# Depthwise convolution of 31 taps as banded block matmuls over four token phases, in a decoder step on eight cores

## The reference

```python
h = rms_norm(x, g_mix)
z = h @ w_in                                   # 2048 -> 10752 columns
glu = z[..., :2048] + b_glu
u = glu[..., :1024] * sigmoid(glu[..., 1024:])
# conv branch: 31 taps back in time, one filter for each of 1024 channels
uc = concatenate([u_past, u], axis=1)
y = depthwise_conv(uc, w_dw) + b_dw            # y[t, c] = sum_j uc[t + j, c] * w_dw[j, c]
y = silu(layer_norm(y, ln_g, ln_b))            # over the 1024 channels
conv_out = y @ w_pw + b_pw
# and q, k, v with rotary positions, three dilated attentions, their mix o_att
x = x + (sigmoid(z_gc) * conv_out + sigmoid(z_ga) * (o_att @ w_o_att)) @ w_out
x = x + (silu(hf @ w_gate) * (hf @ w_up)) @ w_down      # hf = rms_norm(x)
```

## Time and profile before

| | |
|---|---|
| median of three runs | 2172.33 us |
| the profiled execution | 2170.49 us |
| span of its slowest core (core 1), first to last instruction | 2168.6 us |
| spans of the eight cores | 2164.3 to 2168.6 us |
| granted TensorE clock, share of full, each core | 0.989 to 0.990 |
| TensorE matmul busy | 2060.5 us, 95% |
| VectorE / ScalarE busy | 706.2 us, 33% / 432.2 us, 20% |

### The profile page before, as it was taken

The page is one execution under the profiler, slowest core; times in us unless marked ns, Lnnn a source line. Parts: engine busy times, 40 slices in busy tenths (PEclk is TensorE's granted clock), DMA queues, the critical chain, the costliest instruction groups (busy, mean ns, idle before and its releaser), DMA issues.

```text
span 2168.6 us, 34938 instructions; the slowest of 8 cores (2164.3 to 2168.6 us)
## 1 busy us (share of the span) xinstructions
PE 2060.5 (95%) x13809; PEld 1277.3 (59%) x13809; DVE 706.2 (33%) x1105; ACT 432.2 (20%) x783; POOL 68.5 (3%) x122
## 2 busy tenths in 40 slices
PE   1599998999999999999999999999999999999997
PEld 0455554665554566666688756565565565665653
DVE  2344334322222332222224332413414314224125
ACT  2533323332222421111103200000010000000013
POOL 0000000000000000000000000000000000000000
PEclk9799999999999999999999999999999999999999
DMA  9144223427849776894382647585495564553423
GB/s 241 64 103 99 55 50 78 101 60 137 144 90 161 126 145 146 126 202 86 59 199 49 120 76 118 84 141 100 83 155 89 92 101 75 88 83 58 80 47 150
DMA packets 43947, 230.91 MB, mean 106 GB/s; under 512 B 5163, under 2 KB 17563, under 8 KB 28403
## 3 DMA queue, kind: packets, MB, share of 16 engines
q0 software_dynamic: 27552, 137.37, 39.9%
q1 hardware_dynamic: 16235, 91.31, 16.4%
HBM read 350.31 MB, written 59.99 MB: 189 GB/s over the span
## 4 chain that ended last, share of the span: by engine, by line
PE 93%; DMA 2%; ACT 2%; DVE 2%; issue 1%; SPq 0%; DVEq 0%; ACTq 0%
PE ps L125 93%; DVE arena L125 2%; ACT arena L125 2%; DMA arena<-xext 1%; DMA arena<-state 1%; ACT L125 0%; SPq L142 0%; DMA y<-arena 0%; DVEq L85 0%; ACTq L85 0%; SPq L85 0%
## 5 line engine op out<-in xcount | busy, mean ns | idle before, releaser
L125 PE MATMUL ps<-arena 128*128 128x512 bf16 (+8 forms) x13809 | 2060.5, 316 | 94.2 <-DVE arena L125 72.1
L125 PEld LDWEIGHTS ps<-arena 128*128 128x128 bf16 (+2 forms) x13809 | 1277.3, 101 | 876.9 <-issue 116.4
L125 DVE TENSOR_TENSOR arena<-ps,arena 128x512 f32<-128x512 f32 (+5 forms) x729 | 413.6, 570 | 912.5 <-PE ps L125 718.2
L125 ACT ACTIVATE arena<-ps 128x347 f32<-128x347 f32 (+2 forms) x285 | 133.6, 478 | 1074.2 <-PE ps L125 1072.7
L125 ACT ACTIVATE arena<-arena 128x2048 bf16<-128x2048 f32 (+6 forms) x140 | 111.8, 804 | 161.5 <-DVE arena L125 137.3
L125 DVE TENSOR_TENSOR arena<-arena 128x1040 f32<-128x1040 f32 (+7 forms) x167 | 122.8, 742 | 35.7 <-ACT arena L125 22.0
L125 DVE SCALAR_TENSOR_TENSOR arena<-ps,arena 128x347 f32<-128x347 f32 (+3 forms) x75 | 43.4, 579 | 275.3 <-PE ps L125 263.0
L125 ACT COPY arena<-ps 128x512 bf16<-128x512 bf16 (+7 forms) x154 | 93.1, 620 | 126.2 <-PE ps L125 124.6
L125 DVE SCALAR_TENSOR_TENSOR arena<-arena 128x2048 bf16<-128x2048 f32 (+5 forms) x36 | 79.2, 2201 | 50.5 <-ACT arena L125 47.6
L125 ACT CAST arena<-ps 128x384 bf16<-128x384 f32 x72 | 37.0, 514 | 178.2 <-PE ps L125 176.6
L125 ACT ACTIVATE arena<-ps,arena 128x357 f32<-128x357 f32 (+4 forms) x42 | 21.6, 515 | 141.1 <-PE ps L125 139.9
(11 more groups left out here) (14 smaller groups left out, 24.3 us busy)
## 6 DMA issues: line engine op xcount, KB each, us to landing
arena<-wgu POOLq DMA_DIRECT2D x44, 1024.0 KB, 10.6
arena<-wgate POOLq DMA_DIRECT2D x16, 1408.0 KB, 17.8
arena<-w_down POOLq DMA_DIRECT2D x11, 2048.0 KB, 25.7
arena<-xext SPq DMA_DIRECT2D x19, 1024.0 KB
arena<-wqkv POOLq DMA_DIRECT2D x9, 2048.0 KB, 22.5
kso<-ck SPq DMA_DIRECT2D x16, 1022.0 KB
vso<-cv SPq DMA_DIRECT2D x16, 1022.0 KB
arena<-wglu POOLq DMA_DIRECT2D x8, 1024.0 KB, 10.4
```

The source lines that it names most:

```text
L125: self.q[eng].append(lambda e, meth=meth, a=a, kw=kw, s=s: getattr(e, meth)(*a, **kw).then_inc(s, 1))
```

## The change

- The convolution. Each 128-channel block is cut into four groups `q` of 32 channels. `glu` writes `u` split in four phases (token mod 4, `uph`), and 16 small DMAs in `glu_end` bring it to a layout in which the partitions are 4 phases x 32 channels (`uP`). Then a 128x128 matrix holds, for a shift of `s` groups of four tokens, the taps between every input and output phase (a block Toeplitz matrix, diagonal in the channels). `conv(n)` becomes 4 groups x 9 shifts = 36 matmuls of 256 columns. The matrices are made on DVE: four multiplies of 128x1152 per block, from `w4` and a mask.
- The sample tokens are convolved on DVE: a multiply, a reduction and a bias of 496 or 16 elements per block.
- The layer norm works in that order (sums with a block matrix `bones`), and 16 DMAs per block bring its output back to `cT`, which now holds the phases one after the other: 256 prompt and 4 sample tokens for each. `gate_mm` part 2 therefore reads `cT` with a step of 260 elements between neighbouring columns.
- The start: identity and gain row are loaded ahead of the first tile, the gain row is spread over the partitions by four matmuls instead of a DMA, each GLU weight load on POOL waits for a tile to have landed, the tables come in final layout (no transposes in `consts`), and two GLU blocks (n = 0 and 1) run inside the tile phase, after tiles 2, 5 and 9.
- The loop goes over n = 2 to 7 with seven halo tiles (two in n = 6); the last convolution moves behind the first q projection of group 2.

The core of the diff:

```diff
@@ glu_end
-            S.op('dve', lambda e: e.tensor_tensor(out=dgv[ui][:, :, :], in0=mkap(identb, [[0, 31], [1, 128]]),
-                                                  in1=mkap(vecT[:, R_WDW + n:R_WDW + n + 1], [[8, 31], [0, 128]]), op=ALU.mult),
-                 ['identb', 'vecT'], ['dg%d' % ui])
+            S.op('act', lambda e: e.copy(out=phases(uph[ui], 186, 78), in_=tok4(u_[:, 0:312])), [uk], [pk])
+            S.op('dve', lambda e: e.tensor_scalar(out=phases(uph[ui], 0, 8), in0=tok4(u_[:, 328:360]), scalar1=hv, scalar2=None, op0=ALU.mult), [uk, 'hv'], [pk])
+            for q in range(4):
+                for f in range(4):
+                    S.dma('sp', uP[ui][32 * f:32 * f + 32, q, :], uph[ui][32 * q:32 * q + 32, f, :], reads=[pk], writes=[Pk])
+            S.op('act', lambda e: e.copy(out=ucb[ui][:, :, 30:34], in_=u_[:, 312:328].rearrange("p (s j) -> p s j", j=4)), [uk], [uc])
+            prod = mkap(sqt[:, 0:1], [[124, 4], [31, 4], [1, 31]])
+            S.op('dve', lambda e: e.tensor_tensor(out=prod, in0=mkap(ucb[ui][:, 0, 0:1], [[34, 4], [1, 4], [1, 31]]), in1=mkap(vecT[:, R_WDW + n:R_WDW + n + 1], [[0, 4], [0, 4], [8, 31]]), op=ALU.mult),
+                 [uc, 'vecT'], ['sqt'])
...
+            for q in range(4):
+                S.op('dve', lambda e: e.tensor_tensor(out=v3(tpw[ui][q], 36), in0=mkap(dmask[:, 0:1], [[0, 36], [1, 32]]), in1=mkap(w4n[:, 36 * q:36 * q + 1], [[1, 36], [0, 32]]), op=ALU.mult),
+                     ['dmask', 'w4'], ['tp%d' % ui])
@@ conv
-            for j in range(31):
-                S.op('pe', lambda e: e.matmul(PS[3][:, :], lhsT=dgv[ui][:, j, :], rhs=ubb[ui][:, j:j + 512], start=(j == 0), stop=(j == 30)),
-                     [dkey_, ukey], [PSK[3]])
...
+            for hf in range(2):
+                bk = 3 + hf
+                for q2 in range(2):
+                    q = 2 * hf + q2
+                    for s in range(9):
+                        S.op('pe', lambda e: e.matmul(PS[bk][:, 256 * q2:256 * q2 + 256], lhsT=tpw[ui][q][:, 128 * s:128 * s + 128], rhs=uP[ui][:, q, s:s + 256], start=(s == 0), stop=(s == 8)),
+                             [tk, Pk], [PSK[bk]])
@@ ln_n
+                for q2 in range(2):
+                    q = 2 * hf + q2
+                    for f in range(4):
+                        S.dma('sp', cT[32 * q:32 * q + 32, n, 260 * f:260 * f + 256], cP[sl][32 * f:32 * f + 32, q2, :], reads=['cP%d' % sl], writes=['cT%d' % n])
@@ gate_mm
-                S.op('pe', lambda e: e.matmul(PS[pb_ + part][:, 0:nc_], lhsT=wv_[:, k0 + k, :], rhs=src[:, k, c0:c0 + nc_], start=(k == 0), stop=(k == nk - 1)),
+                rhs = mkap(cT[:, k, c0 // 4:c0 // 4 + 1], [[1, nc_ // 4], [260, 4]]) if part == 2 else src[:, k, c0:c0 + nc_]
+                out = tok4(PS[pb_ + part][:, 0:nc_]) if part == 2 else PS[pb_ + part][:, 0:nc_]
+                S.op('pe', lambda e: e.matmul(out, lhsT=wv_[:, k0 + k, :], rhs=rhs, start=(k == 0), stop=(k == nk - 1)),
@@ the start and the tile phase
+        GLU_AT = {2: 0, 5: 1, 9: 2}
...
+            if ti in GLU_AT:
+                for n in range(2):
+                    glu(n, GLU_AT[ti])
+                    if ti == 9:
+                        glu_end(n)
```

More of the change, by code:

```diff
@@ L388, in build_program @@
         S.op('dve', lambda e: e.memset(onesb, 1.0), [], ['onesb'])
+        S.op('act', lambda e: e.activation(out=rs[0], in_=onesf[:, 0:1], func=AF.Ln), ['onesf'], ['rs0'])
         S.op('dve', lambda e: e.tensor_copy(out=identb, in_=identf), ['identf'], ['identb'])
[L392 to L397, removed]
+        after('pool', XBK[0])
         glu_load(0)
+        after('pool', XBK[2])
         glu_load(1)
+        for j in range(4):
+            S.op('pe', lambda e: e.matmul(PS[j][:, :], lhsT=onesf[0:1, :], rhs=gbc[0:1, 512 * j:512 * (j + 1)], start=True, stop=True), ['onesf', 'gbc'], [PSK[j]])
+        for j in range(4):
+            S.op('act' if j % 2 else 'dve', (lambda e: e.copy(out=gbc[:, 512 * j:512 * (j + 1)], in_=PS[j][:, :])) if j % 2 else
+                 (lambda e: e.tensor_copy(out=gbc[:, 512 * j:512 * (j + 1)], in_=PS[j][:, :])), [PSK[j]], ['gbc'])
         QKVW = {'q': 8192, 'k': 0, 'v': 4096}
@@ L484, in consts @@
[L484 to L490, removed]
+            for i in range(2):
+                state_load(i)
@@ L574, in build_program @@
         tile_load(NFIRST + 1)
-        glu_end(0)
-        S.alias(['y%d' % n for n in range(8)], XBK)
-        glu_load_next = 2
-        for n in range(1, 8):
-            ht = NFIRST + n - 1
+        glu_load(3)
+        glu_load(4)
+        S.dma('sp', convs_d[:, 0:26, :], state_d.rearrange("(s r) c -> s r c", r=30)[:, 4:30, :], writes=['convs'])
+        S.alias(['y%d' % n for n in range(8)] + ['yS'], XBK)
+        ht = NFIRST
+        for n in range(2, 8):
             tile_norm(ht)
-            if n + 1 < 8:
-                glu_load(n + 1)
             glu(n, 0)
+            if n == 2:
+                conv_out(0)
+                conv(0)
             conv_out(n - 1)
@@ L596, in build_program, with conv_last @@
                 qkv_load(2, 'k')
-        conv_out(7)
-        conv(7)
-        S.alias(['Wv'], ['dg0', 'dg1'])
-        qkv_load(2, 'v')
+        assert ht == len(tiles)
+        def conv_last():
+            conv_out(7)
+            conv(7)
+            S.alias(['Wv'], ['tp0', 'tp1'])
+            qkv_load(2, 'v')
         o = R0
```

266 lines of the change are left out of this document (167 added, 99 removed).

## The result

The changed kernel takes 2717.84 us (2713.47 to 2909.53) against 2172.01 us of the kernel before: a ratio of 1.2506, with an interval of 1.2481 to 1.2530. The profiled execution of after has a span of 2718.8 us on core 1, against 2168.6 us. So it is slower, as forecast, but by 546 us where I said 118, and far outside my range. Some executions of the kernels were disturbed and longer (such a one is the 2909.53); ratios and readings are of the others, of which e3_before_step260 has one, as have the three kernels of e4, which ran once each.

The account below looks back on a forecast made before the run. TensorE bounds it, busy 2060.5 of 2168.6 us. 2168.6 − 25 (start) − 38 (loop) − 9 (last convolution) + 0 (layer norm) + 190 (gates) = 2286.6, with 3.7 outside the span 2290 us; range 2095 to 2320.

Parts of the forecast that it names:

- The start: Tile phase: first transposes at 16 us, first two GLU blocks through at 97 us for 122.6; gain 25 us.
- `uP`: Small transfers of each block: 16 issues at 0.35 us and a landing, under 10 us, hidden by an iteration.
- The loop: Convolution loop: 24.7 us an iteration, six together 155 us against 193.6 now; gain 38 us.
- the chain I wrote down: Loop, from one glu(n,2) end to the next through ScalarE, DVE and TensorE: 23.4 us, with handovers 24.7 us.
- rival (d): Loop: DVE bounds more, 30 us an iteration as now, 2320 us; chance 0.07, shared with a mixture near the old time.
- The loop's first iteration: First of the six loop iterations, with two convolutions: 28 us.
- The layer norm: Layer norm in group 2, with 16 DMAs (5.6 us of SP) per block: change 0, between −6 and +10 us.
- Part 2 of the gates: 384 matmuls reading cT at 520-byte steps: 1.85 ns a column, 642 ns each instead of 147, +190 us.
- DVE's row: Price for part 2 of the gates from DVE's strided output: 1.875 ns an element, +193 us, the upper bound.
- the row of the weight loads: Price for part 2 of the gates from TensorE's strided weight loads: 0.34 ns a column, +45 us; argued too cheap.
- Rival (c): Gates: as forecast, and starved matmuls let the clock fall to 1.2 GHz, +125 us, 2415 us; chance 0.08.
- The sum: Whole kernel: 2168.6 − 25 − 38 − 9 + 0 + 190 = 2286.6 us; the attention's end forecast at 711.8 us.

Follow-up runs that it names:

- e3_before_step260: The kernel before, with part 2 of the gates reading cT at a step of 260 columns, token groups 348, 348 and 344: 2402.34 us.
- e4: Three kernels: the kernel before with the moving operand of part 2 read at a step of 8, 4 and 2 elements: 2399.75, 2234.45 and 2175.83 us.
- e1_keys: The changed kernel with a key of its own for each small transfer into uP and cT: 2449.76 us, ratio to before 1.1239.
- e8_tp_late: e7_fmajor with the four multiplies that make the Toeplitz matrices moved behind conv(n-1): 2197.27 us, ratio 1.0116.
- e12_halo_first: e10_split_ln with the halo norm earlier, half of uP's transfers by POOL, and the first two halo loads ahead of the small transfers: 2177.17 us.
- e14_two_cps: e12_halo_first with the rotation tables loaded ahead of glu_end(7)'s transfers and two staging tiles for the convolution's state output: 2160.14 us, ratio 0.9942.
- e10_split_ln: e8_tp_late with half of the layer norm's 128 small transfers issued by the POOL queue instead of SP: 2186.33 us, ratio 1.0062.
- e15_pairs: e14_two_cps with the layer norm done in pairs of blocks, 64 small transfers instead of 128: 2155.98 us, ratio to before 0.9920.
- e4_before_step4: The kernel before with the moving operand of part 2 of the gates read at a step of 4 elements (8 bytes): 2234.45 us.
- e7_fmajor: e1_keys with part 2 of the gates reading each phase contiguously, the eviction on VectorE restoring token order: 2217.71 us, ratio 1.0176.

## Why the prediction was wrong

**The start** was right: first transposes at 20 us for 16, `glu(1,2)` through at 102.6 us for 97; gain 20 us for 25.

**`uP`, "16 issues at 0.35 us … under 10 us", hidden.** This is the step that failed. I took the price from four stores to DRAM in a row, which write under four keys, and did not look at the keys of the new ones. A transfer that writes the same key waits for the one ahead to land, 1.72 us, and the queue behind it waits too. It failed three times: in the start of the loop (the halo loads), in each iteration, and in the layer norm, where "16 DMAs (5.6 us of SP) per block" were 27 to 29 us. Keys of their own gave back 271 us of the stage ahead of the gates (reciprocal 1098.4 to 827.7 us). Even then an issue cost 0.61 to 0.69 us here, not 0.35.

**The loop.** In after it took 29 to 49 us an iteration, because of the transfers. Freed of them (e1_keys) the chain I wrote down, through DVE's multiplies, the evictions and the norm, is what the trace shows: TensorE waits some 7 us for DVE ahead of a `tile_T`. The size was still off: 30 us an iteration, rival (d)'s number, not 24.7. Two terms are missing. The first is ScalarE's cast that writes the phases, for which DVE waits 1.76 us. The second is the clock, which I had only in the range and not in the sum: behind each wait TensorE runs at 1.2 GHz at first, so the transposes take 1.8 us for 0.9 and `glu(n,2)` 7.0 for 4.86, together some 3 us. DVE's wait, and the stretches of the transposes and of `glu(n,2)`, in e1_keys:

```profile
215.84 0.30 DVE L125 TENSOR_SCALAR arena<-arena 128x32 bf16<-128x32 f32 x1 [1.76 <-ACT arena L125]
233.80:236.20 2.40, 1.87 (x17) 0.50 0.08 17
236.20:243.20 7.00, 7.00 (x34) 0.71 0.44 151
```

Writing phases is dear on both engines: a multiply of `glu(n,0)` or `glu(n,1)` that does it costs 1.76 us and the cast 1.57, where a contiguous multiply of the same size is 0.59. The two multiplies stand behind the norm, where TensorE waits for DVE only 0.47 us. Three rows of after, VectorE and ScalarE:

```profile
183.31 1.76 DVE L125 SCALAR_TENSOR_TENSOR arena<-ps,arena 128x356 bf16<-128x356 f32 x1 [0.62 <-DMA convs<-arena]
196.47 0.59 DVE L125 SCALAR_TENSOR_TENSOR arena<-ps,arena 128x360 f32<-128x360 f32 x1 [3.49 <-PE ps L125]
197.15 1.57 ACT L125 CAST arena<-arena 128x312 bf16<-128x312 f32 x1 [0.85 <-DVE arena L125]
```

In after the clock was 0.76 on the mean from 181.5 to 457 us. With the matrices moved out of the chain the iteration fell to some 26 us (e8_tp_late).

**The loop's first iteration.** I gave it 28 us and saw in the diff neither the one staging tile (12.6 us) nor the place of the halo loads behind 32 issues; one hid the other, so that the loads' move gave 6 us for 25 to 30 as long as the tile was single (e12_halo_first, e14_two_cps).

**The layer norm, "I take 0, between −6 and +10".** From 457 to 1098 us after needs 641 us; that is where TensorE's waits of 43.1 and 99.4 us lie. Most of it was the serial transfers; with keys, SP's issues still bounded it (e10_split_ln: 20 us ahead of the gates). In e15_pairs the waits for DVE between 300 and 460 us still sum to 26.8 us, against 10.7 in before from 330 to 460 us.

**Part 2 of the gates.** The mechanism was right and the size close: 588 ns for the forecast 642, 1.69 ns a column for 1.85, 169 us for 190. DVE's row was the right neighbour, and the row of the weight loads underrated it, as argued. The remaining 70 us of the 238 are the clock, and the matmuls around the strided ones pay them: 505 of the other matmuls of the gates start 288 ns apart instead of 147, which is 70 us. The strided ones do not notice it: their starts lie 587 ns apart at either level of the clock. Three stretches of after: a strided group, other matmuls behind such a group, and others at full clock:

```profile
1347.90:1352.59 4.69, 4.69 (x11) 1.00 0.00 0
1158.16:1162.20 4.04, 4.04 (x15) 0.50 0.43 56
1150.05:1152.82 2.77, 2.77 (x21) 1.00 0.25 18
```

**Rival (c), the clock.** I gave it 0.08 and it happened, at somewhat over half its price (70 us for 125). "Here it has an instruction running" was no protection: TensorE was busy for all of the 556 us, and the granted clock was 0.83 on the mean. Where the strided matmuls took 308 ns instead of 588 it stayed at 1.00 (e4_before_step4). So the second effect came with the first and was not a case of its own.

**The sum, in after's own terms.** Against the forecast the reciprocal came 387 us late (1098.4 − 711.8). By the reciprocals of the runs: keys 271, matrices 20, layer norm queues 20, halo loads and tables 15, staging tiles 15, pairs 5; the norm's move cost 1 and the turned read 7. These are 338 us of it, each measured on top of the others, so their split depends on the order. They are read on the slowest core, and the eight cores of one execution have this point 4 to 12 us apart; so the items under 10 us are not clear of that, and the 7 us of the turned read are nothing but the choice of the core (the middle ones of the eight have it at some 830 us in e1_keys and in e7_fmajor). Some 49 us are not recovered: e15_pairs has its reciprocal at 760.6 us where I forecast 711.8. Of these 6 lie in the start (103.0 us for 97), 6 in the first iteration (34.2 for 28), 4 in the other five (131 for 127) and 16 in the longer waits for DVE in the layer norm. Four more are a slip of my sum: the 193.6 us of today's loop run to the end of `conv(6)`, my 155 only to `glu(7,2)`, and the 3.9 us of `conv(6)` stand in no term behind it. The rest, 13 us, I did not take apart. And an earlier end of the gates isn't kept whole: in e10_split_ln and from e12_halo_first on the last stage takes 1072.0 to 1074.6 us on the slowest core for 1064.6 in e8_tp_late, and between 0 and 10 us more on the others. There the x tiles for the residual, loaded when the gates end, land after the first results are there (the last row of e15_pairs above). What holds those loads I have not tested.

## What to carry to other kernels

Before you price a transfer by its neighbours, look at what the scheduler makes it wait for: two writes to different partitions under one name are serial, at the price of a landing each, and all that the queue holds behind them is late as well. Many small transfers are priced by issues (here 0.6 to 0.7 us each on SP), so count them before their bytes. A wait of the busiest engine costs more than its length: here the clock was halved behind it, 3 us on top of 7. A moving operand should have its 16-byte pieces full: turning the two loops of the access pattern round and leaving the scatter to the eviction bought back 232 us of 2450.

## What the runs showed of the hardware

- A moving operand costs 1.77 ns for each 16-byte piece that it touches in a row, if that is more than its columns: 347 columns take 148, 154, 308 and 611 ns at a step of 2, 4, 8 and 16 bytes. At 520 bytes, four phases in turn, it is a little less, 588 ns (1.69).
- The granted clock went to and fro between its two levels, 1.2 and 2.4 GHz, while TensorE was busy without a gap: 0.83 to 0.87 of 2.4 GHz on the mean of the gates, where 8 of every 44 matmuls took 588 or 611 ns each; 1.00 where they took 308. Strided matmuls took the same 587 ns at both levels, contiguous ones of 348 columns 288 and 147.
- Transfers of 16 KB between partitions of SBUF: 0.61 to 0.69 us an issue on SP, 1.72 to 1.81 us each when every one waits for the one before to land. Stores to DRAM took 0.35 us an issue in the same queue.
- 87 contiguous elements and a jump, as in e7_fmajor, cost nothing that the stage shows: 317.3 us for the gates, as in before.
